# Three tiles to a head, gates in the row of paired tiles: moving mLSTM's output-gate and SiLU tiles

## The reference

```
q, k, v, ig, fg, og, z = split_cols(pa, A_SIZES)
state, h = run_segments(mlstm_step, state, (q, k, v, ig, lf), segments)
h = ((h - mean(h)) * rsqrt(var(h) + EPS)) * mlstm_norm        # per head of 128
ya = h * sigmoid(og) * silu(z)
merged = ga * (ya @ w_proj_a) + gb * (yb @ w_proj_b) + gc * (yc @ w_proj_c)
x' = x + rmsnorm(merged @ w_out)
```

## Time and profile before

| | |
|---|---|
| median of 3 runs | 2391.26 us (2389.59 to 2392.84) |
| the profiled execution, its own time | 2397.15 us |
| its span, first to last instruction | 2395.3 us |
| mean granted TensorE clock | 0.994 of full speed |
| PE, DVE, ACT busy | 2330.2, 1244.1, 761.7 us |

### The profile page before, as it was taken

The page is one execution under the profiler, slowest core; times in us unless marked ns, Lnnn a source line. Parts: engine busy times, 40 slices in busy tenths (PEclk is TensorE's granted clock), DMA queues, the critical chain, the costliest instruction groups (busy, mean ns, idle before and its releaser), DMA issues.

```text
span 2395.3 us, 46302 instructions
## 1 busy us (share of the span) xinstructions
PE 2330.2 (97%) x19429; PEld 2249.1 (94%) x19429; DVE 1244.1 (52%) x1862; ACT 761.7 (32%) x1138; POOL 47.9 (2%) x71
## 2 busy tenths in 40 slices
PE   5999999999999999999999999999999999999998
PEld 5999999999999999999989989988999999999998
DVE  4444433444387765734536527445646654445354
ACT  5311212112133333323323223233323343324443
POOL 0000000000000000000000000000000000000000
PEclk9999999999999999999999999999999999999999
DMA  5232222222223334112112112131212235444465
GB/s 166 72 125 76 70 88 86 79 80 69 81 81 126 122 104 177 54 47 89 59 47 101 46 47 79 47 133 65 94 71 70 88 117 190 151 147 154 156 208 184
DMA packets 59843, 242.17 MB, mean 101 GB/s; under 512 B 8242, under 2 KB 15588, under 8 KB 39524
## 3 DMA queue, kind: packets, MB, share of 16 engines
q1 hardware_dynamic: 59700, 239.97, 29.4%
HBM read 212.13 MB, written 27.81 MB: 100 GB/s over the span
## 4 chain that ended last, share of the span: by engine, by line
PE 83%; DVE 8%; issue 4%; ACT 2%; DMA 2%; SPq 1%; DVEq 0%; POOL 0%; ACTq 0%; POOLq 0%
PE acc L888 53%; PE acc L1404 6%; PE acc L1035 6%; PE branch L1035 3%; PE branch L1129 2%; PE branch L1404 2%; PE branch L1167 2%; DVE scratch L2091 1%; DVE w_lo L1890 1%; ACT w_hi L1451 1%; DMA w_raw<-in_w_stream 1%; PE branch L1122 1%; PE branch L1312 1%; DMA scratch<-in_x_all 1%; DVE scratch L2500 1%
## 5 line engine op out<-in xcount | busy, mean ns | idle before, releaser
L888 PE MATMUL acc<-act_hi,w_hi 128*128 128x320 f32 (+2 forms) x3776 | 1152.5, 305 | 9.2 <-DVE w_lo L1890 7.3
L888 PE MATMUL acc<-act_lo,w_hi 128*128 128x320 f32 (+2 forms) x3776 | 1120.7, 297 | 0.0
L888 PE MATMUL acc<-act_hi,w_lo 128*128 128x320 f32 (+2 forms) x3776 | 1119.9, 297 | 0.0
L888 PEld LDWEIGHTS acc<-act_hi,w_hi 128*128 128x128 f32 x3776 | 713.5, 189 | 25.6 <-DVE w_lo L1890 8.7
L888 PEld LDWEIGHTS acc<-act_lo,w_hi 128*128 128x128 f32 x3776 | 713.8, 189 | 0.7
L888 PEld LDWEIGHTS acc<-act_hi,w_lo 128*128 128x128 f32 x3776 | 713.3, 189 | 0.0
L1890 DVE TENSOR_TENSOR w_lo<-w_raw,w_hi 128x2048 fp32r<-128x2048 f32 x149 | 341.1, 2289 | 384.4 <-ACT w_hi L1451 383.8
L1451 ACT ACTIVATE w_hi<-w_raw 128x2048 fp32r<-128x2048 f32 x149 | 285.7, 1917 | 183.4 <-PE branch L1404 118.9
L1404 PE MATMUL acc<-act_lo,w_hi 128*128 128x288 f32 x384 | 114.0, 297 | 2.8 <-issue 2.8
L1404 PE MATMUL acc<-act_hi,w_lo 128*128 128x288 f32 x384 | 113.7, 296 | 0.0
L1404 PE MATMUL acc<-act_hi,w_hi 128*128 128x288 f32 x384 | 113.6, 296 | 0.0
(11 more groups left out here) (445 smaller groups left out, 2794.8 us busy)
## 6 DMA issues: line engine op xcount, KB each, us to landing
w_raw<-in_w_stream SPq DMA_DIRECT2D x150, 1024.0 KB, 4.9
w_raw<-in_w_stream SPq DMA_DIRECT2D x40, 512.0 KB, 6.4
gate_logits<-gate_out SPq DMA_DIRECT2D x48, 288.0 KB, 2.1
scratch<-gate_logits SPq DMA_DIRECT2D x48, 288.0 KB, 3.1
scratch<-in_x_all SPq DMA_DIRECT2D x9, 512.0 KB, 5.8
branch_rows<-branch_out SPq DMA_DIRECT2D x16, 288.0 KB, 2.2
scratch<-in_x_all SPq DMA_DIRECT2D x3, 1024.0 KB, 10.7
out_y_prompt<-scratch SPq DMA_DIRECT2D x6, 512.0 KB, 2.9
```

Source lines behind the costliest of these rows:

```text
L888: last = mm(acc[s][:, at:at + hi - lo], a[:, s, w], b[:, k, lo:hi], start=(k == order[0] and a is whi and b is xh), stop=(k == order[-1] a ...
```

## The change

The heads keep three tiles each (k, v, q). The chain of a head runs one head behind: `scores` and `values` stand in the next head's k tile, `carried` in its v tile, `turn_h` at the start of its q tile, and `turn_kv` ahead of block 8 of the q tile. The first two heads are taken out of the loop; the chain of the last head runs in the first three plain tiles. VectorE no longer forms gates there: it copies the turned unit rows to `ybuf`, and they are stored in `yspill`.

The 16 output-gate and z tiles become 8 more pairs of the row, at the odd places; the merge-gate tiles have `PLAIN = 6` whole tiles and 9 pairs at the even places (17 pairs in all). For an odd pair ScalarE takes sigmoid(z) into `side_row` and VectorE multiplies z, the norm's weight and sigmoid(z) (`silu`); SyncE then loads the head's unit rows from `yspill` over `side_row`. In the next pair ScalarE takes sigmoid(og), VectorE multiplies the two gates (`both`) and then the unit rows (`y`), and SyncE stores the result back to `yspill`.

```diff
-A_RUN = A_TILES - A_GATES
+A_RUN = 3
...
-PLAIN = 4
-N_PAIRS = (N_G - PLAIN) // 2
-SHORT = 2 * N_PAIRS
+PLAIN = 6
+N_PAIRS = (N_G - PLAIN) // 2 + NH_A
+SHORT = NH_A * (A_TILES - A_RUN) - PLAIN
...
+    return A_AT + t // A_GATES * A_TILES + A_TILES - A_GATES + t % A_GATES
+
+
+def out_gates(p):
+
+    return p // 2 if p % 2 else None
+
+
+def pair_tiles(p):
+
+    i = out_gates(p)
+    if i is None:
+        return gate_tile(PLAIN + p), gate_tile(PLAIN + p + 1)
+    return A_AT + A_TILES * i + A_RUN, A_AT + A_TILES * i + A_RUN + 1
+
+
+def pairs_before(p, gates):
+
+    return sum((out_gates(q) is None) == gates for q in range(p))
...
-    if p == N_PAIRS - 1 and m >= 5:
-        return m - 3
+    if p == N_PAIRS - 1 and m >= 4:
+        return (2, 3, 2)[m - 4]
...
+    "row_sigmoids": """
+        z o""",
+    "row_gates": """
+        silu both y""",
...
+        side_row = first_tmp[1].rearrange("p a b -> p (a b)")
...
+            def head_out(i):
+
+                sp.wait_ge(*A_["mlstm_scalar"].after(i, "state_out"))
+                sp.dma_start(c_p[bass.ds(i, 1)].rearrange("a v k -> (a v) k"), c_out[:, 0, :]).then_inc(states_out, 16)
+                sp.dma_start(c_s[bass.ds(i, 1)].rearrange("a v k -> (a v) k"), c_out[:, 1, :]).then_inc(states_out, 16)
+                sp.wait_ge(*A_["mlstm_vector"].after(i, "y"))
+                sp.dma_start(yspill[bass.ds(i, 1)].rearrange("a p t -> (a p) t"), ybuf[:, 0:KEPT]).then_inc(y_out, 16)
...
+                        if i:
+                            sp.wait_ge(*A_["mlstm_tensor"].after(i - 1, "k_turned"))
...
+                    if j == 2 and i:
+                        head_out(i - 1)
...
+            def gated_out(i):
+
+                sp.wait_ge(*R_["gates"].after(i, "y"))
+                sp.dma_start(yspill[i], gbuf[1][:, 0:KEPT]).then_inc(y_gated, 16)
...
+                i = out_gates(p)
+                if i is None:
+                    if p:
+                        gated_out(out_gates(p - 1))
+                    sp.wait_ge(*R_["adds"].after(p, "c21"))
+                    sp.dma_start(graw[PLAIN + p + 1], gbuf[1][:, 0:KEPT]).then_inc(gates_out[1], 16)
+                    sp.wait_ge(*R_["adds"].after(p, "c12"))
+                    sp.dma_start(graw[PLAIN + p], gbuf[0][:, 0:KEPT]).then_inc(gates_out[0], 16)
+                else:
+                    sp.wait_ge(*R_["gates"].after(i, "silu"))
+                    sp.dma_start(side_row, yspill[i]).then_inc(h_here, 16)
...
+            def head(N, i, last=None):
+
+                if last is None:
+                    product(N(0))
+                    product(N(1))
+                    product(N(2), {8: [lambda: turn_kv(N, i)]}, cols=QUERY_COLS)
+                else:
+                    product(N(0), {4: [lambda: scores(last, N(-1))], 12: [lambda: values(last)]})
+                    product(N(1), {6: [lambda: carried(last)]})
+                    product(N(2), {0: [lambda: turn_h(last)], 8: [lambda: turn_kv(N, i, last)]}, cols=QUERY_COLS)
...
+            with looped(pe, 0, NH_A // 2 - 1) as rnd:
+                for one in range(2):
+                    head(lambda j, one=one: Num(A_AT + A_RUN * (2 + one), 2 * A_RUN, rnd, j), pe.snap(rnd * 2 + (2 + one)), pe.snap(rnd * 2 + (1 + one)))
...
+            top = NH_A - 1
+            product(G_AT, {4: [lambda: scores(top, G_AT - 1)], 12: [lambda: values(top)]}, cols=EVEN_COLS)
+            product(G_AT + 1, {6: [lambda: carried(top)]}, cols=EVEN_COLS)
+            product(G_AT + 2, {0: [lambda: turn_h(top)]}, cols=EVEN_COLS)
+            product(G_AT + 3, {2: [turn_n]}, cols=EVEN_COLS)
+            for n in range(G_AT + 4, G_AT + PLAIN):
...
+            def state_out(i, stores=None):
+                act.wait_ge(*G.after(i, "states_turned"))
+                if stores is not None:
+                    act.wait_ge(states_out, stores)
+                S.done(f(c_out[:, :, :].rearrange("p a b -> p (a b)"), bra[:, 0:256], ACT.Copy), "state_out")
+
+            def head(N, i, last=None, stores=None):
                 in_order(N(0), ak, scale=float(P) ** -0.5)
                 split_hi(N(2))
                 in_order(N(1), av)
+                if last is not None:
+                    state_out(last, stores)
                 split_hi(N(3))
...
-                f(split2(aeo[:, 0:KEPT]), source(N(3)), ACT.Exp, scale=-1.0).then_inc(evac_done, 1)
-                split_hi(N(5))
-                src = source(N(4))
-                f(split2(az[:, 0:KEPT]), src, ACT.Copy)
-                f(split2(aez[:, 0:KEPT]), src, ACT.Exp, scale=-1.0).then_inc(evac_done, 1)
-                act.wait_ge(*G.after(i, "states_turned"))
-                S.done(f(c_out[:, :, :].rearrange("p a b -> p (a b)"), bra[:, 0:256], ACT.Copy), "state_out")
-                split_hi(N(6))
-                act.wait_ge(states_out, i * 32 + 32)
...
-            corners_hi(0)
             plain(G_AT, gbuf[0][:, :])
             split_hi(G_AT + 2)
+            plain(G_AT + 1, gbuf[1][:, :])
+            split_hi(G_AT + 3)
+            state_out(NH_A - 1, 32 * (NH_A - 1))
+            corners_hi(0)
+            act.wait_ge(gates_out[0], 16)
+            plain(G_AT + 2, gbuf[0][:, :])
+            split_hi(G_AT + 4)
...
+            def sigmoid_z(i):
+                act.wait_ge(*R_["adds"].after(2 * i + 1, "c21"))
+                if i:
+                    act.wait_ge(*R_["gates"].after(i - 1, "y"))
+                R_["sigmoids"].done(f(side_row, gbuf[1][:, 0:KEPT], ACT.Sigmoid), "z")
+
+            def sigmoid_o(i):
+                act.wait_ge(*R_["adds"].after(2 * i + 1, "c12"))
+                R_["sigmoids"].done(f(gbuf[0][:, 0:KEPT], gbuf[0][:, 0:KEPT], ACT.Sigmoid), "o")
+
             for p in range(N_PAIRS):
                 top = p == N_PAIRS - 1
+                if p and out_gates(p) is None:
+                    sigmoid_o(out_gates(p - 1))
...
+                if out_gates(p) is not None:
+                    sigmoid_z(out_gates(p))
...
-                dve.wait_ge(evac_done, N(4) + 1)
-                gz = aez[:, 0:KEPT]
-                V.done(v.tensor_scalar(gz, gz, 1.0, None, ALU.add), "gate1")
-                own("gate1")
-                V.done(v.scalar_tensor_tensor(out=gz, in0=aeo[:, 0:KEPT], scalar=1.0, in1=gz, op0=ALU.add, op1=ALU.mult), "gate2")
-                own("gate2")
-                V.done(v.reciprocal(gz, gz), "gate3")
-                own("gate3")
-                V.done(v.scalar_tensor_tensor(out=agz[:, 0:KEPT], in0=az[:, 0:KEPT], scalar=pk[:, 25:26], in1=gz, op0=ALU.mult, op1=ALU.mult), "gate")
                 dve.wait_ge(*G.after(i, "h_turned"))
-                own("gate")
-                v.tensor_tensor(ybuf[:, 0:320], brb[:, 0:320], agz[:, 0:320], ALU.mult)
-                V.done(v.tensor_tensor(ybuf[:, 320:KEPT], brb[:, 576:832], agz[:, 320:KEPT], ALU.mult), "y")
-                split_lo(N(6))
-                dve.wait_ge(y_out, i * 16 + 16)
-                dve.wait_ge(*S.after(i, "state_out"))
-                dve.wait_ge(*G.after(i, "states_turned"))
-
-            with looped(dve, 0, NH_A // 2) as pair:
-                head(pair, 0)
-                head(pair, 1)
+                if stores is not None:
+                    dve.wait_ge(y_out, stores)
+                v.tensor_copy(ybuf[:, 0:320], brb[:, 0:320])
+                V.done(v.tensor_copy(ybuf[:, 320:KEPT], brb[:, 576:832]), "y")
...
+            def silu(i):
+                dve.wait_ge(*R_["sigmoids"].after(i, "z"))
+                norm = VEC["mlstm_norm"] + i
+                R_["gates"].done(v.scalar_tensor_tensor(out=gbuf[1][:, 0:KEPT], in0=gbuf[1][:, 0:KEPT], scalar=vecs[:, norm:norm + 1],
+                                                        in1=side_row, op0=ALU.mult, op1=ALU.mult), "silu")
+
+            def both_gates(i):
+                dve.wait_ge(*R_["sigmoids"].after(i, "o"))
+                dve.wait_ge(*R_["gates"].after(i, "silu"))
+                add(gbuf[1][:, 0:KEPT], gbuf[1][:, 0:KEPT], gbuf[0][:, 0:KEPT], ALU.mult, R_["gates"], "both")
+                dve.wait_ge(*R_["gates"].after(i, "both"))
+
+            def gated(i):
+                dve.wait_ge(h_here, 16 * i + 16)
+                add(gbuf[1][:, 0:KEPT], gbuf[1][:, 0:KEPT], side_row, ALU.mult, R_["gates"], "y")
...
+            split_lo(G_AT + 3)
             corners(0)
             corners(1)
-            split_lo(G_AT + 2)
+            split_lo(G_AT + 4)
             corners(2)
-            split_lo(G_AT + 3)
+            split_lo(G_AT + 5)
...
-                dve.wait_ge(gates_out[0], 16 * (PLAIN // 2 + p))
+                if p and out_gates(p) is None:
+                    both_gates(out_gates(p - 1))
+                dve.wait_ge(gates_out[0], 16 * (PLAIN // 2 + pairs_before(p, True)))
                 sum_row(p, "p2", gbuf[0][:, 0:TH], p1_row, "c11")
                 if p:
...
                 sum_row(p, "p5", u5_row, u2_row, "u5")
+                if p and out_gates(p) is None:
```

(45 more changed lines are left out.)

169 lines of the change are left out of this document (69 added, 100 removed).

## The result

The median of the kernel after is 2361.07 us (2360.67 to 2362.03, 4 runs) beside 2390.82 us of the kernel before on the same chip: ratio 0.9875, 95% interval 0.9858 to 0.9892. A second measurement, on another chip, gave 2363.55 us and again 0.9875 (0.9859 to 0.9892). The prediction was 2366.4 us: 24.9 us were forecast, 29.8 us came. The profiled execution took 2361.02 us, and its span is 36.9 us shorter than that of the kernel before, whose profiled execution lay 5.9 us over its median.

What follows compares the result with a forecast made beforehand. The prediction took PE's matmuls to bound the kernel (busy 2330.2 of 2395.3 us). Tiles and pairs -21.4 us, corner work -3.5 us and everything else 0 made -24.9 us, from 2391.26 to 2366.4 us, range 2361 to 2376.

Steps and rivals of the forecast that it cites:

- Tiles and pairs: Heads and row: 14 whole tiles of 12.70 us go, 7 pairs of 22.34 us come, -21.4 us.
- The slower rival: Heads: `turn_h` waits in every head because `h_unit` ends late; decides from 3.1 us per head; slower 5%.
- The corner term: Plain tiles ahead of the row: DVE's corner work starts earlier, so PE waits less; -3.5 us, bounds 0 and -5.4.
- three restarts: Plain tiles: 0.2 us of gain put on each, added to 2.9 us of PE's listed waits.
- The row: Paired tiles: added sigmoids and multiplications fit beside PE's work, 1.1 us to spare before p6; cost 0.
- The first rival, coupling: Row: slow sigmoid and unhidden table load in odd pairs delay `silu`; 9 us given back, 2375; within a 20% case.
- The table: Row: one sigmoid table load, covered by ACT's idle time; perhaps one more after the row, 0 to 1.3 us, taken as 0.
- the coupling case: Row and heads: the row's coupling of DVE to ACT or other small waits, 2371 to 2386 us, 20%.
- the sum: Whole kernel: -21.4 us for tiles and pairs and -3.5 us for the corner work make -24.9 us.

Runs made afterwards that it cites:

- before_no_gates: The kernel before, with VectorE forming no output gates in the heads (unit rows stored as they are); ratio 0.9984 (0.9976 to 0.9993).
- sigmoid_x2: The kernel after, with each sigmoid of z taken twice, one behind the other; 2361.25 us, ratio 0.986 (0.9845 to 0.9876).
- sigmoid_x5: The kernel after, with each sigmoid of z taken five times, one behind the other; 2385.21 us, ratio 0.9965 (0.9952 to 0.9978).
- after_dve_pad: The kernel after, with 70 more empty instructions (satisfied waits) in VectorE's program in the row; 2367.26 us, ratio 0.9892 (0.9877 to 0.9907).
- before_both_pads: The kernel before, with 58 empty instructions added to VectorE's program and 37 to TensorE's; 2389.20 us, ratio 0.9975 (0.9966 to 0.9984).

## Why the prediction was right, and where it was not

**Tiles and pairs: right.** 48.08 us per head where 48.1 was worked out, and 22.34 per pair. The slower rival died with the heads' window: PE full throughout, no wait at `turn_h`.

**The corner term: right.** 3.5 us forecast; 3.8 in the traces and 3.8 in `before_no_gates`. The waits left in the row are 1.5 and 0.2 us, where 1.3 were expected to stay. The prediction didn't see that 1.64 us of DVE's lateness there was a stop for its code; by the 3.35 us that DVE now waits for ACT, the lead from the gates alone would have done, but this is argued and not shown. The 0.2 us for each of three restarts in the 3.5 was my estimate, and no run shows it apart: in `before_no_gates` the listed waits fell by 2.8 us (4.2 to 1.4) and the median by 3.8, within 1.7 to 5.7.

**The row: right, but with less room than counted.** DVE idles as forecast before each `silu`. Timeline of DVE after, as the earlier trace rows:

```profile
671.11 0.82 DVE L2240 SCALAR_TENSOR_TENSOR gate_out<-gate_out,vecs,scratch 128x576 f32<-128x576 f32 x1 [0.75 <-ACT scratch L1688]
...
672.22 1.22 DVE L2163 TENSOR_TENSOR w_lo<-scratch,w_hi 128x1024 fp32r<-128x1024 f32 x1
```

The low part of s2 ends at 673.44. The chain puts the start of p6 at 674.46, which gives the 1.1 us of room that the prediction counted, since it took its own 812.7 from the chain. But PE asks for the first weights of p6 earlier, by PEld's timeline:

```profile
674.15 0.32 PEld L1095 LDWEIGHTS acc<-corner_terms,w_hi 128*128 128x128 f32 x2
```

So the room is 0.7 us, and 0.65 by `sigmoid_x2` and `sigmoid_x5`: the two-fold sigmoid (0.72 us more) just fills it, and the five-fold one overruns it. The first rival, coupling, is real, as the 15.8 us of waits in `sigmoid_x5` show, but it decides only beyond that room. By this room its 9 us would have been 8 x 1.6 = 13.

**The table: right on the path.** Line 1688, the sigmoid of z, has one load for the whole row:

```profile
L1688 ACT ACTIVATE scratch<-gate_out x8: 685/685/686, 581.0 to 893.8; 128x576 f32<-128x576 f32 x8
L1688 ACT ACT_TABLE_LOAD  x1: 1283/1283/1283, 578.7 to 578.7; - x1
```

A sigmoid of 576 columns is 0.69 us where I took 0.68 between bounds of 0.55 and 1.64; three of them would be 2.06 us, more than the 1.64 of 1728 columns at once, so each has a part that doesn't shrink. The load ends at 580.0 and the sigmoid starts at 581.04, when DVE's c21 is done, so nothing waited for the load. Elsewhere in this trace an activation ends at 959.03, a load of 1.28 us starts at 959.04, and the next activation at 960.34: 0.01 us lie ahead of that load and 0.02 behind it, and the switch took 1.31 us in all. The chances let the coupling case reach 2386, where the loads of the earlier trace rows give 2375; no run shows a cost of a switch beyond the load, and the row had one switch, which ACT's idle time covered. In the RWKV loop stand four loads more than before (20 and 16), where I expected one; from its first round to its last, at the same line, it is 482.3 us after and 483.0 before, so they cost nothing.

**Missed, 1 us: the last pair.** I gave the store of y six us. In the last pair c22 needs the buffer from which y is stored, and the product behind the row needs c22. The store is issued at 908.70 and c22 could start at 912.42, 3.7 us later; the store took 4.4. DVE and then PE wait:

```profile
913.30 0.82 DVE L2163 TENSOR_TENSOR gate_out<-acc,scratch 128x288 f32<-128x288 f32 x2 [0.88 <-DMA branch_rows<-gate_out]
```

```profile
914.56 0.41 PE L937 MATMUL acc<-act_hi,w_hi 128*128 128x320 f32 x1 [0.72 <-DVE gate_out L2163]
```

**The step that failed: the sum had no term for the code behind the row.** I took unedited code for unchanged time. The traces put 11.2 us there, and about 6 of them are shown by runs to be DVE's stop: taking it away from the kernel before gave 5.7 us, putting it into the kernel after cost 6.0 (4 by the ratios). With 25.7 us from the edited stages (24.9 were forecast) the 5.7 make 31.4, close to the 29.8 us of the medians. The view that would have told was that of the waits, PE's of the earlier trace rows read to its end and DVE's beside it: an idle time that ends with "issue" in front of a 3.7 us wait was here a cost that an edit ahead of it moved. It should have widened the range downwards by 6 us, since nothing in the trace of before tells where the code would come to stand. Which way it would go was luck: `after_dve_pad` is the same change with the stop in it, and its ratio makes a gain of 25.9 us, within 1 us of the forecast.

The program came in by loads of two sizes: 16.4 KB each on queue q8 (1.75 MB in 107 packets after) and 8 KB on q14 (0.19 MB in 24). The stop doesn't stand at the entry of the HGRN loop: in the trace of before DVE's first record of the loop is at 1588.73 us, and the stop ends 44 records and 26.5 us behind it, beside a load of 8 KB on q14.

**Still open**: 4 to 5 us of the traces' 11.2 (PE's stop at L1404 and the half clock behind it, and a third half-clock stretch at 2178 us), which `before_both_pads` shortens in its trace and not in its median. In all four traces that have it, PE's stop ends 2.4 to 2.5 us behind the start of a 16 KB load on q8, which speaks for its code too but is no test. Open as well: why the stop moved by four instructions and not 16 in `before_no_gates`, and which part of a program shares a piece with which.

## What to carry to other kernels

Price the edited stages from full windows and the room at their tightest order, as here: both terms held to 1 us or so in 25. Take the room from the timeline of the weight loads and not from the chain: here 1.1 us were really 0.65. Then look for idle time that ends with "issue", and for the wait and half clock behind it. In this kernel it depended on how many instructions stood ahead, so an edit before it removed or created it, and a variant that misses its microsecond may have lost it there. Moving the code by some empty instructions helps to tell.

## What the runs showed of the hardware

A stop of DVE of 3.4 to 3.5 us, in which it waited for nothing that the profile shows, came and went with 58 or 70 instructions that do nothing, and cost about 6 us: 3.7 of PE's wait and, as an estimate from the rest, some 2.5 of half clock. It ended 1.7 to 1.8 us behind the start of an 8 KB load of instructions on q14, as did the other stops of DVE behind the row. It stood there with 787 and with 1171 of DVE's instructions ahead of the HGRN loop, 384 apart, and not with 845 or 1101. Eight waits of PE of 2.0 us each in `sigmoid_x5` brought four half-clock stretches of 3.4 us, so 15.8 us of waiting made the row 22.8 us longer.
